# A recurrent transformer block on one core: weight panels cut into three-pass pieces inside the 64x64 inverse

## The reference

```python
u = rms_norm_2(h, mix_norm[l])
(z_s, xbc, dt_s, qkv, z_d, b_d, a_d, gate_s, gate_d) = jnp.split(u @ w_in[l], split_points, axis=-1)
y_s = mamba2_branch(...)     # ends with a norm over 4 groups: yg * rsqrt(mean(yg^2)) * norm_w
y_d = deltanet_branch(...)   # in chunks of 64 tokens: sol = triangular_solve(eye + M, rhs)
merged = sigmoid(gate_s) * (y_s @ ssm_w_branch[l]) + sigmoid(gate_d) * (y_d @ dn_w_branch[l])
```

## Time and profile before

| | us |
|---|---|
| three executions, lowest / median / highest | 2304.49 / 2305.78 / 2311.12 |
| the profiled execution, its own time | 2304.57 |
| its span, first to last instruction | 2302.8 |
| TensorE busy | 2165.9 (94%) |
| VectorE busy | 1338.9 (58%) |
| ScalarE busy | 1158.5 (50%) |
| mean granted TensorE clock | 0.972 |

### The profile page before, as it was taken

The page is one execution under the profiler, slowest core; times in us unless marked ns, Lnnn a source line. Parts: engine busy times, 40 slices in busy tenths (PEclk is TensorE's granted clock), DMA queues, the critical chain, the costliest instruction groups (busy, mean ns, idle before and its releaser), DMA issues. The chain is left out here.

```text
span 2302.8 us, 41405 instructions
## 1 busy us (share of the span) xinstructions
PE 2165.9 (94%) x15844; PEld 1901.6 (83%) x15844; DVE 1338.9 (58%) x1851; ACT 1158.5 (50%) x1703; POOL 61.3 (3%) x74
## 2 busy tenths in 40 slices
PE   6999889999999998998999999999999887999998
PEld 5887778888888987887998887887997787998887
DVE  3436375555557976574555555556896566556554
ACT  3453644445445556743545445444557663535444
POOL 0000000000000010000000000000002000000000
PEclk9999999999999998997999999999999898999999
DMA  9652245545553544321355554554454422254553
GB/s 396 241 223 101 74 153 184 189 175 184 187 195 129 182 142 140 141 75 43 143 184 190 192 190 167 189 193 165 146 183 129 147 92 76 74 183 183 186 194 121
DMA packets 53329, 373.06 MB, mean 162 GB/s; under 512 B 6304, under 2 KB 6304, under 8 KB 9280
## 3 DMA queue, kind: packets, MB, share of 16 engines
q1 hardware_dynamic: 47664, 341.81, 41.2%
q0 software_dynamic: 5520, 29.23, 3.6%
HBM read 369.90 MB, written 1.11 MB: 161 GB/s over the span
## 5 line engine op out<-in xcount | busy, mean ns | idle before, releaser
L1410 ACT ACTIVATE HI<-ring 128x1024 fp32r<-128x1024 f32 x614 | 632.9, 1054 | 788.0 <-PE banks L535 399.3
L1955 DVE TENSOR_TENSOR LO<-ring,HI 128x1024 fp32r<-128x1024 f32 x326 | 398.8, 1225 | 374.1 <-ACT HI L1410 368.6
L1961 DVE TENSOR_TENSOR LO<-ring,HI 128x2048 fp32r<-128x2048 f32 x139 | 318.5, 2291 | 275.7 <-ACT HI L1410 275.6
L499 PE MATMUL banks<-UH,HI 128*128 128x256 f32 x1456 | 427.1, 293 | 0.0
L500 PE MATMUL banks<-UL,HI 128*128 128x256 f32 x1456 | 416.4, 286 | 0.0
L501 PE MATMUL banks<-UH,LO 128*128 128x256 f32 x1456 | 416.0, 286 | 0.0
L533 PE MATMUL banks<-HI,UH 128*128 128x512 f32 x896 | 350.1, 391 | 7.1 <-DVE LO L1961 4.9
L535 PE MATMUL banks<-HI,UL 128*128 128x512 f32 x896 | 349.4, 390 | 0.0
L534 PE MATMUL banks<-LO,UH 128*128 128x512 f32 x896 | 349.2, 390 | 0.0
L499 PEld LDWEIGHTS banks<-UH,HI 128*128 128x128 f32 x1456 | 283.3, 195 | 16.3 <-issue 15.5
L500 PEld LDWEIGHTS banks<-UL,HI 128*128 128x128 f32 x1456 | 283.3, 195 | 1.2 <-issue 1.2
(11 more groups left out here) (323 smaller groups left out, 3093.9 us busy)
## 6 DMA issues: line engine op xcount, KB each, us to landing
ring<-in_w_stream SPq DMA_DIRECT2D x315, 1024.0 KB, 4.8
ARENA<-in_ada_stream POOLq DMA_DIRECT2D x16, 1024.0 KB, 5.1
ARENA<-in_ada_stream SPq DMA_DIRECT2D x8, 1024.0 KB, 14.4
GRMS<-cum_rows POOLq DMA_DIRECT2D x16, 256.0 KB, 3.5
ARENA<-in_na_bias POOLq DMA_DIRECT2D x2, 1024.0 KB, 13.4
RMS<-cum_rows POOLq DMA_DIRECT2D x8, 256.0 KB, 3.4
RSTD<-cum_rows POOLq DMA_DIRECT2D x8, 256.0 KB, 3.6
ARENA<-in_ropes POOLq DMA_DIRECT2D x1, 1088.0 KB, 19.3
```

Source lines behind the costliest of these rows:

```text
L499: nc.tensor.matmul(out, lh, rh, start=start, stop=False, **kw)
L1410: nc.scalar.activation(HI[:, q % PARTS, at], ring[:, q % RING, at], ACT.Copy).then_inc(hi_ready, 1)
L1955: nc.vector.tensor_tensor(LO[:, q % PARTS, at], ring[:, q % RING, at], HI[:, q % PARTS, at].bitcast(F32), ALU.subtract).then_inc(lo_ready, 1)
L1961: nc.vector.tensor_tensor(LO[:, q % PARTS, :], ring[:, q % RING, :], HI[:, q % PARTS, :].bitcast(F32), ALU.subtract).then_inc(lo_ready, 2)
```

## The change

- TensorE: the four halves are gone. In their place the same 32 products of the two gate panels are issued one at a time. `wide_piece` makes one product, three matmuls. In iteration n a piece stands behind v(n) and another behind turn(n-1), from n = LEVEL_FIRST = 2 to n = 17, 32 pieces in all. The matmuls and their number are the same. Each piece waits for `lo_ready` of its panel, as each half did.
- ScalarE: `late_gate(L_ZD)` stands ahead of the copy of unit 10 instead of 8, `late_gate(L_ZD + 1)` ahead of that of unit 18 instead of 16.
- VectorE: `group_norm(g)` is taken apart. Its reciprocal stands behind unit 4g, two of the four scalings behind unit 4g+1, the other two behind 4g+2. `late_low` stands behind units 11 and 19 instead of 10 and 18.

```diff
-LEVEL_PANELS = {3: (L_ZD, 0), 7: (L_ZD, 1), 11: (L_ZD + 1, 0), 15: (L_ZD + 1, 1)}
+LEVEL_FIRST, LEVEL_PIECES = 2, 4 * KT
@@ TensorE
+            def wide_piece(w, q, rounds, par, e, k):
+
+                src = both(panel(q, rounds), lambda x: tiles(x, KT))
+                if e + k == 0:
+                    pe.wait_ge(wide_free, w + 1)
+                mm = product(bank[4 + par][:, e * S:(e + 1) * S], both(src, lambda x: x[:, k, e * P:(e + 1) * P]), u_parts(k),
+                             start=(k == 0), stop=(k == KT - 1))
+                if e == 1 and k == KT - 1:
+                    mm.then_inc(panel_used, 2)
...
+                def level_piece(s):
+
+                    j = L_ZD + s // (2 * KT)
+                    if 0 <= s < LEVEL_PIECES:
+                        wide_piece(w0 + L_CONV + L_ZS + j, Q_LAYERS + LQ_WIDE + L_CONV + L_ZS + j, rounds, j % 2,
+                                   s // KT % 2, s % KT)
...
                 for n in range(UNITS_DN):
                     inverse_v(n)
+                    level_piece(2 * (n - LEVEL_FIRST))
                     if n + 2 < UNITS_DN:
                         inverse_u(n + 2)
                     if n:
                         inverse_turn(n - 1)
-                    if n in LEVEL_PANELS:
-                        late_wide(*LEVEL_PANELS[n])
+                    level_piece(2 * (n - LEVEL_FIRST) + 1)
@@ ScalarE
-                    if n == 8:
+                    if n == LEVEL_FIRST + 8:
                         late_gate(L_ZD)
-                    if n == 16:
+                    if n == LEVEL_FIRST + 16:
                         late_gate(L_ZD + 1)
@@ VectorE
-                def group_norm(g):
+                def group_reciprocal(g):
                     dve.wait_ge(yrms_ready, 4 * l + g + 1)
-                    need(step(nc.vector.reciprocal(GRMS[:, g, :], GRMS[:, g, :])))
-                    for e2 in range(4):
+                    return step(nc.vector.reciprocal(GRMS[:, g, :], GRMS[:, g, :]))
+
+                def group_scaled(g, part):
+                    for e2 in (2 * part, 2 * part + 1):
...
                     if n + 2 < UNITS_DN:
                         inverse_masked(n + 2)
-                    if n in (10, 18):
-                        late_low(L_ZD + (n - 10) // 8)
-                    if n % 4 == 3 and n < 4 * GROUPS:
-                        group_norm(n // 4)
+                    g = n // 4
+                    if g < GROUPS and n % 4 == 0:
+                        inverted = group_reciprocal(g)
+                    elif g < GROUPS and n % 4 in (1, 2):
+                        if n % 4 == 1:
+                            need(inverted)
+                        group_scaled(g, n % 4 - 1)
+                    elif n == 11:
+                        late_low(L_ZD)
+                    elif n == 19:
+                        late_low(L_ZD + 1)
```

More of the change, by code:

```diff
@@ L2448, in group_norm @@
                                                              ALU.mult, ALU.mult)
-                    ins.then_inc(ys_ready, 1)
+                    if part:
+                        ins.then_inc(ys_ready, 1)
                 def qk_reciprocal(i):
```

## The result

Six executions of each kernel gave a median of 2311.39 us for the changed kernel (2307.98 to 2312.99) and of 2303.11 for the kernel before (2300.19 to 2311.12, the first three of them being those that the forecast started from). The ratio is 1.0039, interval 1.0027 to 1.0050. By the ratio that is 9.0 us (6.2 to 11.5) slower (the two medians differ by 8.3), inside the stated range, clear of no change, and 6.7 us more than the +2.3 of the forecast. The forecast's 2308 us looks closer than that, 3.4 us off, only because the three further executions of the kernel before took its median from 2305.78 down to 2303.11. A second comparison gave 1.0043 (1.0030 to 1.0057).

What follows compares the result with a forecast made beforehand. The prediction took latency to bound the bursts before and TensorE's own pace, 2.18 us an iteration, after; the stages summed to +0.6 us, one clock fall made +2.3, giving a 2308 us median, range 2300 to 2318.

Steps and rivals of the forecast that it cites:

- the likeliest sum: Both layers' stages together: +0.6 us at the full clock, +2.3 us with one fall of the clock; chance 0.62.
- within 0.3%: Whole kernel: time within about 0.3%, 7 us, of the kernel before, not to be told from no change; chance 0.78.
- the clock: TensorE behind the waits at v(2): one fall of 3.4 us in the two layers, costing at most 1.7 us.
- 0.31 us for a change of shape: TensorE, from 64x64 bursts to full matmuls and back: 0.31 us for every piece, making an iteration 2.18 us.
- VectorE's slack: VectorE beside the pieces: from unit 4 on the divided norm costs nothing, its reciprocal fitting by 0.06 us.
- The first reciprocal: VectorE behind unit 0, no pieces beside it: v(2) goes 1.75 us later in each layer, TensorE waiting.
- The gate: ScalarE's first gate, now behind copy 9: 0.75 us of TensorE's waiting left of 2.35.
- u(17): TensorE's stall ahead of u(17), 0.82 and 1.37 us: kept, as the number of instructions ahead is the same.
- The tail: From v(18) to `last_u`, second gate ahead of copy 18: 6.46 us, +0.13 and +0.33 in the two layers.
- The rival on the clock: Clock at 1.2 GHz after v(2)'s wait and at the gate, both layers, 6.8 us each: +14.2, 2320 us; chance 0.15.
- the argument from the 0.82 us: Against the clock falling more: the 0.82 us stall before u(17) in the second layer brought no fall.

Runs made afterwards that it cites:

- Twelve- and six-pass pieces: Changed kernel with pieces of four products (twelve passes, eight a layer, norm two units later): 0.9990; with pieces of two (six passes, 16 a layer): 0.9996.
- the divided norm alone: Kernel before with only the group norm divided, reciprocal behind units 0, 4, 8, 12, halves and gates as before: 1.0027, +6.2 us.
- the filled one: Changed kernel with eight added full matmuls, result unused, between turn(0) and v(2), where TensorE otherwise waits: 2309.07 us, 1.0036.

## Why the prediction was right, and where it was short

The range held and the sign of the likeliest sum was right, but 0.78 of the chances stood on "within 0.3%": the ratio of 1.0039 lies outside that, though its interval reaches in to 1.0027. Of the 9.0 us the forecast named 2.3. What was too small is one term, the clock, and a part of the rest stays open. Step by step:

- **0.31 us for a change of shape, TensorE's own pace as the bound.** Right: the iteration was 2.18 by the sum and is 2.11 to 2.12 (u to turn is 0.28 and the turn's own path to the piece 0.34 instead of 0.40). Twelve- and six-pass pieces confirm the price. That the array itself asks it, and not the instructions around it, remains the prediction's assumption; no run separates the two.
- **VectorE's slack.** Right: no wait for it in units 5, 9 and 13. Without the division it waits 1.6 us behind two of the norms of a layer and more behind the other two.
- **The first reciprocal.** Mechanism right, size a little over: v(1) to v(2) is 2.70, where 3.04 was worked out. Update(1) starts 0.09 us before the reciprocal's recorded end, not 0.04 behind it.
- **The gate.** 0.75 us of waiting forecast, 0.67 measured at turn(11) in both layers.

```profile
1941.53 0.46 PE L1243 MATMUL banks<-CON,ARENA 64*64 64x64 f32 x16 [0.67 <-ACT ARENA L1825]
```

- **u(17).** Kept by the forecast, and kept by the kernel, though in another place: in the middle of v(15), behind its tenth matmul. What it kept is the number of instructions ahead of it, which was the reason given; the last section counts them.
- **The tail.** 6.46 forecast, 6.78 measured from v(18) to `last_u`, with 3.06 us of waiting for ScalarE's gate and copy:

```profile
1961.14 0.71 PE L1243 MATMUL banks<-CON,ARENA 64*64 64x64 f32 x16 [3.06 <-ACT ARENA L1830]
```

- **The clock: the term that was too small.** The forecast took one fall of 3.4 us in the two layers, at 1.7 us. The five stages of the changed kernel in which the clock held behind v(2) are 46.08 to 46.68 us, mean 46.25; the other three are 54.87, 51.09 and 47.63. Over four profiles the stages of both layers are 92.8, 100.9, 97.4 and 93.7 us, mean 96.2, against 90.6 in the two of before: +5.6. Of it 1.9 are there without any such fall (the 0.6 of the sum, against a profile that stood 1.2 above the mean of the two), and 3.7 are these three stages (in the first of them the clock fell a second time, behind v(15), whose next two units took 3.58 and 3.59). The price per us was right (3.55 instead of 2.11 for the one short fall, 1.44 against 1.7). The number of falls was about right too (three in eight stages, where one in two was taken). Wrong was how long a fall lasts: 13.7 us where the longest row used was 6.80. In the second profile of the changed kernel TensorE's records from 1020.80 on are without a gap for those 13.70 us and the clock still stays down. The trace of before could have warned. It has falls of 13.7 us, at the last merge of either layer, and in the first layer a fall right behind the 1.37 us ahead of u(17), which the argument from the 0.82 us of the second layer left out:

```profile
1052.80:1056.20 3.40, 3.40 (x44) 3.28 (x36) 3.04 (x5) 0.38 (x1) 0.00 (x0) 0.50 0.02 5
1063.00:1076.60 13.60, 10.74 (x140) 9.93 (x133) 2.74 (x4) 6.06 (x20) 0.00 (x0) 0.50 0.22 78
```

- **The rival on the clock** stood at 0.15 and 2320 us. Its mechanism is what happened, at v(2) and not at the gate, in some executions, so with less than half of its price. The argument against it, that bursts alone hold 1.00 with a wait in each unit, does not cover a wait of 1.2 us and more. The Trainium skill, "TensorE: Matmul & The Clock Gate", section on psum-queue depth-cycling, says that frequent short idle times make the clock oscillate; the changed kernel's drains alone didn't, at 1.00 for 13 us in five of eight stages. It took one longer wait.

Counted over all profiles of kernels with the wait of 2.70 at v(2) and nothing in it (the changed kernel, six passes, the divided norm alone), the clock fell behind v(2) in 6 of 12 stages. In the kernels without that wait, and in the filled one, it fell there in none of 16. Pauses of the kind told of in the last section, and the one ahead of u(17), point the same way: behind those of 1.2 to 1.8 us the clock fell in 5 of 14 cases, behind the 11 of 0.5 to 1.1 us in none. Of the 11 us that moving the reciprocal by two units was worth, 2.8 are its own wait and 3.7 the falls behind it, by the means of the profiles. The other 5 are not explained by them.

**What stays open.** The span outside the two stages is 2213.4 us on average in the four profiles of the changed kernel (2207.4 to 2217.8) and 2210.0 in the ten of all others (2206.0 to 2211.8). Two or three us of the difference are thus not in the stages. Among the changed kernel's own four profiles this time goes with the clock: 2217.8 us with 120 us at the lower level outside the stages, 2215.0 and 2213.4 with 113, 2207.4 with 106. But such stretches differ between two profiles of one kernel too, and no run settles whether the change has a part in them. Nor is it shown why the filled wait gave back so little.

## What to carry to other kernels

Before work is cut finer to fill idle time, read from the trace what one change between the two kinds of matmul costs, and set it against the idle time that one piece fills: here 0.36 us of idle time in a unit against 0.31 us for each piece. Two three-pass pieces in a unit cost more than that, one six-pass piece a little less; alone the six-pass pieces came out level with the kernel before, and 0.14% under it once the first reciprocal had moved. A filler moved away from long work on another engine uncovers it: look where the first slice of that work now stands with nothing beside it. And where TensorE has become the bound, a wait can cost more than itself: here 2.8 us of waiting in two layers brought another 3.7 through the clock. So the waits go first and the fine cut second.

## What was not expected of the hardware

TensorE stood still inside a burst. In all eight stages of the changed kernel it paused for 0.78 to 1.33 us behind the tenth matmul of v(15), with no semaphore to wait for between the 16 matmuls of a burst:

```profile
1948.63 0.34 PE L1233 MATMUL banks<-SQ,ARENA 64*64 64x64 f32 x6 [1.32 <-issue]
```

With eight matmuls and a wait more ahead of it, the pause moved to behind the first matmul of v(15) in both layers, nine matmuls earlier. With TensorE's stream left as it is and only VectorE's norm moved by two units, it stood in u(19) in both layers:

```profile
1053.98 0.33 PE L1218 MATMUL banks<-ARENA 64*64 64x64 f32 x4
1055.13 0.45 PE L1218 MATMUL banks<-ARENA 64*64 64x64 f32 x12 [0.82 <-issue]
```

The place goes by the number of instructions. Counted from TensorE's last branch ahead of the stage (weight loads, matmuls and the instructions that wait), the first record behind the pause is the 4760th in all eight stages of the changed kernel and in both layers with the eight matmuls added, and the 5016th, 256 later, with the norm moved. The pause ahead of u(17) in the kernel before ends at the 4760th too (4759th in the second layer). In the 14 profiles there are 32 places in these bursts at which two neighbouring matmuls start more than 0.2 us apart. They lie at 3736, 3992, 4248, 4760 and 5016, always a multiple of 256 from each other. So TensorE's stream is held up at the borders of blocks of 256 instructions, and which border shows depends on the timing. That the next block arrives late there is the likely reading, but no run shows what is late. The Trainium skill, "Runtime: NRT & Kernel Launch", section on instruction fetch, says that fetching ahead hides behind the pace at which instructions are issued. If that is what these pauses are, the rows differ, by 0.5 to 1.8 us each for those told here.
